# Three modulation tiles of VectorE moved from the query latent's tiles into retention heads 1 to 3

## What is computed

```python
c_act = jax.nn.silu(c)
mod = (c_act @ w_mod[l] + b_mod[l])[:, None, :]
sh1, sc1, g1, sh2, sc2, g2 = jnp.split(mod, N_MOD, axis=-1)
h = rms_norm(x, norm1_w[l]) * (1.0 + sc1) + sh1
```

## Time and profile before

| | |
|---|---|
| Median of 3 runs | 1345.79 us (1344.12 to 1351.33) |
| The profiled execution's own time | 1348.65 us |
| Its span, first to last instruction | 1346.8 us |
| Granted TensorE clock, mean of the span | 0.987 of full speed |
| PE busy | 1298.9 us, 96% |
| DVE busy | 808.1 us, 60% |
| ACT busy | 612.3 us, 45% |
| POOL busy | 48.6 us, 4% |

### The profile page before, as it was taken

The page is one execution under the profiler, slowest core; times in us unless marked ns, Lnnn a source line. Parts: engine busy times, 40 slices in busy tenths (PEclk is TensorE's granted clock), DMA queues, the critical chain, the costliest instruction groups (busy, mean ns, idle before and its releaser), DMA issues. The chain is left out here.

```text
span 1346.8 us, 24698 instructions
## 1 busy us (share of the span) xinstructions
PE 1298.9 (96%) x9416; PEld 1130.7 (84%) x9416; DVE 808.1 (60%) x1461; ACT 612.3 (45%) x1047; POOL 48.6 (4%) x85
## 2 busy tenths in 40 slices
PE   6999999999999998999999999999999989999897
PEld 5999999999999998789999989989999954444344
DVE  6476557588766667467888757858645742222214
ACT  4545545544444544555544446656534441211112
POOL 0100020000000000000000000000000000000100
PEclk8999999999999999999999999999989999999999
DMA  9774355566667553235667776432123599999992
GB/s 372 171 247 161 126 175 179 178 219 220 219 220 242 196 184 129 79 109 188 234 229 232 256 245 215 157 109 79 64 94 125 172 396 369 416 418 418 418 419 104
DMA packets 83286, 295.77 MB, mean 220 GB/s; under 512 B 11062, under 2 KB 12086, under 8 KB 83056
## 3 DMA queue, kind: packets, MB, share of 16 engines
q1 hardware_dynamic: 72720, 263.68, 54.1%
q0 software_dynamic: 10464, 30.66, 7.8%
HBM read 287.76 MB, written 11.53 MB: 222 GB/s over the span
## 5 line engine op out<-in xcount | busy, mean ns | idle before, releaser
L2087 DVE TENSOR_TENSOR ring_low<-ring,w_hi 128x1024 fp32r<-128x1024 f32 x292 | 355.2, 1223 | 191.0 <-ACT w_hi L1605 190.3
L816 PE MATMUL bank<-hn_hi,w_hi 128*128 128x272 f32 (+1 forms) x1416 | 413.1, 292 | 4.4 <-DVE hn_low L2108 3.9
L820 PE MATMUL bank<-hn_hi,ring_low 128*128 128x272 f32 (+1 forms) x1416 | 406.6, 287 | 0.0
L819 PE MATMUL bank<-hn_low,w_hi 128*128 128x272 f32 (+1 forms) x1416 | 405.8, 287 | 0.0
L1605 ACT ACTIVATE w_hi<-ring 128x1024 fp32r<-128x1024 f32 x292 | 302.4, 1051 | 114.2 <-PE bank L816 105.9
L816 PEld LDWEIGHTS bank<-hn_hi,w_hi 128*128 128x128 f32 x1416 | 269.7, 190 | 8.2 <-DVE hn_low L2108 4.4
L819 PEld LDWEIGHTS bank<-hn_low,w_hi 128*128 128x128 f32 x1416 | 269.8, 191 | 0.3
L820 PEld LDWEIGHTS bank<-hn_hi,ring_low 128*128 128x128 f32 x1416 | 270.0, 191 | 0.0
L816 PE MATMUL bank<-arena_r,w_hi 128*128 128x256 f32 (+1 forms) x816 | 234.8, 288 | 4.5 <-DVE ring_low L2087 2.1
L820 PE MATMUL bank<-arena_r,ring_low 128*128 128x256 f32 (+1 forms) x816 | 232.9, 285 | 0.0
L819 PE MATMUL bank<-arena_r,w_hi 128*128 128x256 f32 (+1 forms) x816 | 232.4, 285 | 0.0
(11 more groups left out here) (458 smaller groups left out, 1590.1 us busy)
## 6 DMA issues: line engine op xcount, KB each, us to landing
ring<-weights SPq DMA_DIRECT2D x396, 512.0 KB, 3.5
mod_part<-mod_rows POOLq DMA_DIRECT2D x40, 512.0 KB, 4.7
tab<-weights SPq DMA_DIRECT2D x32, 512.0 KB
arena<-weights SPq DMA_DIRECT2D x29, 512.0 KB, 14.5
w_late<-weights SPq DMA_DIRECT2D x28, 512.0 KB
tab<-tables SPq DMA_DIRECT2D x1, 2858.0 KB, 17.5
skew<-arena POOLq DMA_DIRECT2D x1, 2048.0 KB, 46.7
expert_rows<-mod_part POOLq DMA_DIRECT2D x4, 512.0 KB, 31.3
```

What stands on the lines that cost most here:

```text
L816: begun = mm(dst[:, 0:cols], wh, high(k), start=k == 0, stop=False)
L819: mm(dst[:, 0:cols], wh, low(k), start=False, stop=False)
L820: last = mm(dst[:, 0:cols], wl, high(k), start=False, stop=k == K - 1)
L2087: tt_(ring_lo[:, slot, :], ring[:, slot, :], w_hi[:, n % SPLITS, :], ALU.subtract).then_inc(S("w_lo_ready"), 1)
```

## The change

DVE runs one `mod_tile()` in each of heads 1, 2 and 3, after the low parts up to gate tile 1 and before it waits for the `av` tiles; the three in the query latent's loop are gone. The wait for `c_silu` comes with them. ACT runs the Silu of `c_row` in head 1 in place of head 2. POOL loads row blocks 1 to 3 of `w_mod` before the 16 bias loads, each when the tile before it is used; row blocks 4 to 39 follow them as before. The number of tiles and of loads is the same, and each later tile takes the row block three further on.

```diff
--- before.py
+++ after.py
@@ -758,7 +758,10 @@
             pool.dma_start(c_row, c_rows).then_inc(rel_loaded, 16)
             pool.wait_ge(rows_moved[0], 32)
             pool.wait_ge(rows_moved[1], 32)
-            pool.dma_start(mod_row, mod_rows[0:P, :]).then_inc(mod_loaded, 16)
+            for n in range(RH):
+                if n:
+                    pool.wait_ge(mod_used, n)
+                pool.dma_start(mod_row, mod_rows[n * P:(n + 1) * P, :]).then_inc(mod_loaded, 16)
             pool.wait_ge(S("skew_written"), 16)
             pool.wait_ge(S("decayed"), RH)
             pool.wait_ge(S("roped"), 2 * RH)
@@ -767,7 +770,7 @@
                 for off, lo, n in ((255, 0, P), (127, P, SEQ)):
                     pool.dma_start(bias_a[:, a, lo:lo + n],
                                    bass.AP(skew.tensor, a * flat + off, [[511, P], [1, n]])).then_inc(S("bias_loaded"), 16)
-            for n in range(1, MOD_TILES):
+            for n in range(RH, MOD_TILES):
                 pool.wait_ge(mod_used, n)
                 pool.dma_start(mod_row, mod_rows[n * P:(n + 1) * P, :]).then_inc(mod_loaded, 16)
             pool.wait_ge(S("bias_loaded"), 16 * 2 * AH)
@@ -1691,7 +1694,7 @@
                     act.wait_ge(vec_loaded, 16)
                     fn(wba_hi[:, :], V("wba", 0, DT * 8), ACT.Copy).then_inc(S("wba_hi_ready"), 1)
                     fn(small[:, 0:DT], V("c", 0, DT), ACT.Silu).then_inc(S("c_silu"), 1)
-                if hh == 2:
+                if hh == 1:
                     act.wait_ge(rel_loaded, 32)
                     fn(c_row, c_row, ACT.Silu).then_inc(S("c_silu"), 1)
                 for d in range(4):
@@ -2217,6 +2220,9 @@
                     stt(a, total.to_broadcast([hi - lo, RDV]), -1.0 / RDV, a, ALU.mult, ALU.add)\
                         .then_inc(S("v_centred"), 1)
                 lows(gate_tile(hh, 1))
+                if hh:
+                    dve.wait_ge(S("c_silu"), 2)
+                    mod_tile()
                 wait_stored(dve, at["av", hh])
                 for d in range(1, 4):
                     wait_stored(dve, at["av", hh] + d)
@@ -2353,7 +2359,6 @@
                         lambda k: ckv_lo[:, k, :], lambda k: V("kva", k), KVT, T0)
             for t in range(3, QT):
                 lows(at["qa"] + t)
-                mod_tile()
             for t in range(3):
                 lows(vm_tile(t))
             norm_scale("cq", SEQ)
```

## The result

The changed kernel takes 1341.49 us (median of 13 runs, 1338.12 to 1347.76), the kernel before 1345.79 (13 runs). The ratio is 0.9969 with a 95% interval of 0.9955 to 0.9983: 4.2 us less, 2.3 to 6.1. Forecast were 1339.7 us and 6.1 us less, with most weight on a gain of 5.0 to 6.7.

What follows compares the result with a forecast made beforehand. PE's dense products were taken to bound the kernel, with DVE the late engine at the latent. From the median 1345.79 us, 0 in the heads, -6.1 at the latent and 0 elsewhere gave 1339.7 us; range 1336.4 to 1344.6.

Steps and rivals of the forecast that it cites:

- The heads cost nothing: Heads 1 to 3: DVE's tiles and ACT's Silu hidden by PE's `av` tiles, 0 us; 4.9 us without that cover.
- The latent: Query latent, three tiles removed: reciprocal 6.8 us sooner, limited by PE's root, and `qr1` at 511.0, 6.1 us sooner.
- Transfers and POOL: Loads in the heads: `c_row` 6.8 us early, row block 0 1.9 us early, bias loads near 193; cost 0.
- The clock at the latent: PE's `qr` at full clock saves 1.49 us; the wait before `qr1` on DVE's rotation grows from 1.17 to 1.6 us.
- the larger gain of 7.65 us: Rival at the latent: the wait before `qr1` shrinks towards none, up to 7.65 us gained, 1338.1 us; chance 0.34.
- The rival in which the clock falls in the new gap: Before `qr1`, 1.6 us idle among transposes: clock falls to half, 1.49 us lost, 1341.2 us; chance 0.10.
- the page's rule as I had used it here: Before `qr1`: transposes not counting as busy for the clock gate speaks for a clock fall; sum then 1341.2 us.
- Every later event 6.1 us sooner: After the latent: the whole 6.1 us shift lasts to the end of the profile.
- three signs of being wrong: Head 1 grows; `qr1` starts after 512.5 or before 510; the shift at 517 is not there at the end.
- the expert stage: Late stage, forecast at 0 as it moves with PE; rival: transfers bound it, gain lost, 1345.8 us, chance 0.05.
- The slower rival: Head 1: `c_row` and row block 0 land late, over 0.5% slower, 1353.3 us at 16 us delay; chance 0.05.
- L - 2.4: Head 1: cost in us if writes ahead on POOL's queue take L us longer; gain gone at L = 8.5.

Runs made afterwards that it cites:

- Addition alone: Changed kernel with the three modulation tiles at the latent kept too, 43 tiles in all: 1346.25 us, ratio 0.9992 to the kernel before.
- removal alone: Kernel before without the latent's three modulation tiles and their loads, nothing added to the heads: 1341.22 us, ratio 0.9958.
- work and no waits: Kernel before, tiles kept at the latent, row blocks of the second and third not loaded: 1343.13 us, ratio 0.9982; 1340.63 us when repeated.
- the second execution of the kernel before: Kernel before profiled again without edit, for its clock: own time 1355.14 us, the slowest of all.
- the late loads: Changed kernel with `c_row` loaded three times one after the other: 1345.43 us, ratio 0.9987; same loads in the kernel before as control: 1346.38 us.

## Why the prediction was right

**The heads cost nothing**: right. The tile of head 1 was to run from 102.3 with 0.5 us to spare; in the times of the trace before it ran from 102.2 with 0.6. Addition alone and removal alone agree on it.

**The latent**: right, step by step, again in the times of the trace before (0.54 us added). The reciprocal at 497.56 (forecast 497.5), the split's end at 505.15 (505.1 to 505.6), `qr1` at 511.05 (511.0), 1.71 us idle before it (1.6). That the root from PE is late next, so that not all of DVE's 10.5 us arrive, shows in the 1.41 us of wait before the reciprocal. That the three tiles' work fits into DVE's waits there, so that the gain comes with the waits for row blocks alone, was not said; the run with work and no waits shows it.

**Transfers and POOL**: right. Bias loads at 192.94 against "near 193", without effect.

**The clock at the latent**: its place in the accounts was wrong, the sum was not. I let the end of half clock bring 1.49 us, and let the new wait take it back. In the run with the addition alone PE has full clock and gains nothing, since `qr1` waits for DVE's rotation either way. So the larger gain of 7.65 us would have needed that chain to go. The rival in which the clock falls in the new gap was priced rightly, if the fall comes at `qr1`: the second execution of the kernel before lost 1.47 us so, where I had 1.49. In the changed kernel it did not come: all nine traces in which DVE does not wait for row blocks at the latent have 1.00 from 490 to 530 us, seven with 1.71 us idle before `qr1` and two with 0.94. With 2.10 us idle it fell in one of three traces. The Trainium skill ("TensorE: Matmul & The Clock Gate", Part 4: PE-mode transpose) has transposes not count as busy in the way of other matmuls. With 1.47 us of transposes and 1.71 idle from 507.33 on, the clock stayed at 1.00, so by the page's rule as I had used it here the forecast would have been worse; the rule itself was not tested.

**"Every later event 6.1 us sooner"**: wrong for the first profile, where 2.6 us were left at the end; this is one of the three signs of being wrong that the prediction itself names. On the mean it is nearly right. The gain is whole at the second block and then meets a scatter that I had not priced, up to 8.5 us in the stage from z to the scatter, with 6.8 to 27 us at the low clock. I had it as a half sentence in the rival of the larger gain. Behind it comes the expert stage, which I put at nothing for the forecast and which is 0.5 to 2 us longer in most executions that reach it early. Over all 25 runs of the changed kernel and all 74 of the kernel before, the means are 1341.3 and 1347.1 us: 5.9 us. The forecast's 1339.7 is below the first median of 1341.49, and its starting point is not the reason: the median of its three runs, 1345.79, is also that of the 13. The 1.8 us lie with the changed kernel, of which 5 of the first 13 runs, and none of the 12 others, took over 1344 us. Their mean granted clocks are 0.984 to 0.987, those of the 20 others 0.987 to 0.992. How near the mean of all runs comes to the forecast is in part luck, as the clock and the expert stage were not in the sum.

**The slower rival** did not happen, and the late loads show that it names the right loads but takes the price from the wrong engine. With row block 0 landing at 109.0 in the times of before, 8.6 us late, L - 2.4 gives 6.2 us. DVE's first addition of squares was 6.1 us late indeed, but PE does not wait for it. PE was 4.9 us late, by 3.34 us of wait for ACT, which had waited 6.41 us for `c_row`, and by 1.6 us for the clock. So the margin that counted is the 6.8 us of `c_row`; what a late row block alone costs was not run. In all three traces of the changed kernel the row block was in time (head 1 is 45.52 us behind head 0 in each).

## What to carry to other kernels

A helper task inside an idle stretch costs nothing by its work as long as the work fits there; here it was the wait for its data that made it late. The three tiles would have been free at the latent, had their row blocks been there, and with 6.9 us of transfer waits in DVE's in-order program they cost 6.0 us of the kernel. Move such a task where the same queue has a head's length between uses, and check the margins of the first loads, each on the path by which the bounding engine would feel it. Compare two traces from a common instruction, stage by stage; a total of one execution says little when the spread between executions is as large as the gain. Look at the mean granted clock that each run lists as well: over the 25 runs of the changed kernel it goes with the time (correlation -0.91).

## What the runs showed of the hardware that was not expected

TensorE's granted clock does not fall at the same moments in each execution of one and the same kernel. In the second block the time at 0.50 between 885 and 1105 us was 10.2, 13.7 and 27.3 us in three executions of the kernel before, and 10.2, 13.6 and 27.2 in three of the changed one. The stage from z to the scatter was 215.4 to 221.6 us long with it, a spread as large as what the change gives. The moments are not free either: in 14 traces they form three patterns, each seen with the latent's waits and without. Nor are they places where PE idles long: from 960 to 1030 us PE was busy for 69.81 of 70 us in every execution whose rows are shown, at a clock of 0.95, 0.88, 1.00 and 0.88. The stretch from 530 to 890 us had 0 to 3.4 us at 0.50 in every trace. What selects the pattern is not known.
